# Attention scores laid out with keys on partitions, reduced over the keys by GpSimd

## The reference, cut to what matters

```python
def swa_sink_attention(q, k, v, sinks, rel_bias):
    # chunks of 64 queries; each reads its own and the previous chunk of 64 keys (a band of 128)
    logits = jnp.einsum('bnqkgd,bnskd->bnkgqs', q, kb).astype(jnp.float32)
    logits = logits * (1.0 / math.sqrt(HEAD_DIM)) + band_bias(rel_bias)[None, None]
    logits = jnp.where(valid[None, :, None, None, None, :], logits, NEG)
    sink = sinks.astype(jnp.float32).reshape(1, 1, N_KV_HEADS, GROUP, 1, 1)
    m = jnp.maximum(jnp.max(logits, axis=-1, keepdims=True), sink)
    p = jnp.exp(logits - m)
    denom = jnp.sum(p, axis=-1, keepdims=True) + jnp.exp(sink - m)
    p = (p / denom).astype(vb.dtype)
    o = jnp.einsum('bnkgqs,bnskd->bnqkgd', p, vb)
    return o.reshape(b_, s_, ATTN_WIDTH)
# afterwards: attn * silu(g_attn), next to conv * silu(g_conv), times w_out
```

## Time and profile before

| | |
|---|---|
| time, median of 3 runs | 1341.59 us (1341.4 to 1342.21) |
| the profiled execution | 1342.15 us, span 1340.4 us |
| PE busy | 1327.5 us, 99% of the span |
| DVE busy | 908.1 us, 68% |
| ACT busy | 543.5 us, 41% |
| POOL busy | 90.3 us, 7% |
| units of attention | 393 to 965 us of the span |

### The profile page before, as it was taken

One profiled execution on the slowest core, in us unless ns is written; L12 is line 12 of the kernel. 1 busy time (PEld: TensorE's weight loads), 2 busy tenths in 40 slices (PEclk: granted clock), 3 DMA queues, 4 the chain that ended last, 5 costly groups with the idle time before them and its releaser, 6 DMA issues.

```text
span 1340.4 us, 16528 instructions
## 1 busy us (share of the span) xinstructions
PE 1327.5 (99%) x6038; PEld 1099.2 (82%) x6038; DVE 908.1 (68%) x1132; ACT 543.5 (41%) x946; POOL 90.3 (7%) x151
## 2 busy tenths in 40 slices
PE   9999999999999999999999999999999999999997
PEld 8887888888888888888888888888888888888886
DVE  6899766323577449975589745997439896665376
ACT  7856532232233433434334333334323444321444
POOL 1222220000000000000000000000001121100001
PEclk9999999999999999999999999999999999999999
DMA  9779995988797998779987799787898978899768
GB/s 368 288 271 373 389 351 150 319 310 318 290 297 241 308 301 277 230 219 317 302 287 249 235 312 305 225 261 244 295 348 296 326 259 287 298 306 360 267 260 301
DMA packets 167888, 390.01 MB, mean 291 GB/s; under 512 B 77920, under 2 KB 90240, under 8 KB 146176
## 3 DMA queue, kind: packets, MB, share of 16 engines
q1 hardware_dynamic: 148272, 322.08, 71.7%
q0 software_dynamic: 18240, 62.92, 12.8%
q10 hardware_dynamic: 1296, 3.96, 0.8%
HBM read 294.18 MB, written 98.93 MB: 293 GB/s over the span
## 4 chain that ended last, share of the span: by engine, by line
PE 91%; DVE 6%; issue 2%; DMA 1%; ACT 0%; POOL 0%; POOLq 0%; DVEq 0%; ACTq 0%
PE banks L2009 86%; PE banks L2038 1%; PE banks L2050 1%; DVE x_main L1357 1%; DVE w_ring L1344 1%; DMA x_park<-e 1%; PE banks L1969 1%; PE banks L2059 1%; PE banks L2060 1%; DVE raw L1454 0%; PE banks L1994 0%; DVE raw L1442 0%; DVE e L1502 0%; DVE raw L1436 0%; DVE z L1466 0%
## 5 line engine op out<-in xcount | busy, mean ns | idle before, releaser
L2009 PE MATMUL banks<-x_main,w_ring 128*128 128x512 f32 x2352 | 551.0, 391 | 1.0 <-DVE e L1505 0.5
L2009 PEld LDWEIGHTS banks<-x_main,w_ring 128*128 128x128 f32 x2352 | 438.5, 188 | 91.9 <-issue 1.4
L970 ACT ACTIVATE w_ring<-raw 128x1024 fp32r<-128x1024 f32 x223 | 235.5, 1056 | 544.4 <-PE banks L2009 537.6
L1344 DVE TENSOR_TENSOR w_ring<-raw,w_ring 128x1024 fp32r<-128x1024 f32 x223 | 272.9, 1224 | 218.3 <-ACT w_ring L970 216.7
L2009 PE MATMUL banks<-x_far,w_ring 128*128 128x512 f32 x1680 | 393.4, 391 | 0.1
L2009 PEld LDWEIGHTS banks<-x_far,w_ring 128*128 128x128 f32 x1680 | 313.0, 188 | 64.7 <-DVE e L1502 0.5
L2009 PE MATMUL banks<-w_ring,x_main 128*128 128x512 f32 (+1 forms) x1020 | 230.9, 387 | 0.3 <-DVE e L1502 0.3
L2009 PEld LDWEIGHTS banks<-w_ring,x_main 128*128 128x128 f32 x1020 | 189.9, 188 | 39.6 <-DVE e L1502 0.7
L505 POOL DMA_DIRECT2D x_park<-x_main x104 | 56.1, 539 | 1006.0 <-DVE x_main L1357 1005.9
L1001 ACT ACTIVATE x_main<-z 128x512 fp32r<-128x512 f32 x104 | 64.9, 624 | 116.6 <-issue 81.5
L1357 DVE TENSOR_TENSOR x_main<-z,x_main 128x512 fp32r<-128x512 f32 x104 | 71.3, 687 | 37.7 <-ACT x_main L1001 37.5
(11 more groups left out here) (164 smaller groups left out, 845.3 us busy)
## 6 DMA issues: line engine op xcount, KB each, us to landing
x_far<-x_park SPq DMA_DIRECT2D x84, 1024.0 KB, 6.3
x_main<-x_park SPq DMA_DIRECT2D x84, 1024.0 KB, 6.1
raw<-in_w_blocks_dram SPq DMA_DIRECT2D x127, 512.0 KB, 5.4
x_park<-x_main POOLq DMA_DIRECT2D x104, 512.0 KB, 5.7
q_cur<-qkv_park SPq DMA_DIRECT2D x64, 128.0 KB, 4.9
z<-mix_park SPq DMA_DIRECT2D x16, 512.0 KB, 7.7
z<-in_x_dram SPq DMA_DIRECT2D x6, 1024.0 KB, 13.0
x_park<-e POOLq DMA_DIRECT2D x8, 512.0 KB, 6.4
```

What stands on the lines that cost most here:

```text
L970: act.activation(w_ring[:, n % NW, :, 0, :], raw[:, c, k:k + 2, :], ACT.Copy).then_inc(w_hi_ready, 1)
L1344: dve.tensor_tensor(w_ring[:, n % NW, :, 1, :], raw[:, c, k:k + 2, :], w_ring[:, n % NW, :, 0, :], ALU.subtract).then_inc(w_lo_ready, 1)
L2009: op = pe.matmul(bank, left, right, start=(first and i == 0), stop=(kt == HK - 1 and i == 2), skip_group_check=goes_on)
```

## The change

Scores are computed with the 128 keys on the partitions and 8 heads times 64 queries along the row (128x512), so the probabilities come out as the product with the values wants them, and the transposes on PE go. The maximum over the keys and the sum over the keys now run across partitions, by GpSimd's `partition_all_reduce`. The sink is a second block of 512 columns beside the scores. The output is not normalised through the probabilities: the gate is multiplied by the reciprocal of the sum, which DVE gets by transposing 32x32 blocks. The low part of the probabilities goes from DVE to POOL, ahead of the sum. The order by `o`: DVE scales at 1, POOL takes the maximum at 1, DVE shifts by it at 4, ACT takes the exponential at 5 and the high part at 6, POOL the low part and the sum at 5, DVE weights the gate at 11.

```diff
+        logits = [sb(f"logits{i}", [P, 2, N], Z + 4096 + 4096 * i) for i in range(KVH)]
+        probs = sb("probs", [P, 2, N], Z + 12288)
+        top = sb("top", [P, N], Z + 16384)
+        total = sb("total", [P, N], Z + 18432)
...
+            def key_max(u):
+                pool.wait_ge(logits_read, u + 1)
+                if u > 0:
+                    pool.wait_ge(shift_step, 2 * u)
+                pool.partition_all_reduce(top, logits[u % 2][:, 0, :], P, bass.bass_isa.ReduceOp.max).then_inc(max_ready, 1)
+
+            def split_p_lo(u):
+                pool.wait_ge(pt_hi_ready, u + 1)
+                pool.tensor_tensor(pt_lo[:, :], probs[:, 0, :], pt_hi[:, :], ALU.subtract).then_inc(pt_lo_ready, 1)
+
+            def key_sum(u):
+                pool.wait_ge(exp_done, u + 1)
+                if u > 0:
+                    pool.wait_ge(weight_step, 6 * u)
+                pool.partition_all_reduce(total, probs[:, 0, :], P, bass.bass_isa.ReduceOp.add).then_inc(key_sum_ready, 1)
...
+                act.wait_ge(shift_step, 2 * u + 2)
+                act.activation(probs[:, :, :], probs[:, :, :], ACT.Exp).then_inc(exp_done, 1)
...
+                act.activation(pt_hi[:, :], probs[:, 0, :], ACT.Copy).then_inc(pt_hi_ready, 1)
...
+            def scale_logits(u):
...
+                dve.scalar_tensor_tensor(out=logits[kv][rows, 0, :], in0=logit_ps[rows, :], scalar=SCALE,
+                                         in1=bias[rows, kv * PAIRS * 2:(kv + 1) * PAIRS * 2, :].rearrange("p h s -> p (h s)"),
                                          op0=ALU.mult, op1=ALU.add).then_inc(logits_read, 1)
...
+            def shift_logits(u):
...
+                dve.wait_ge(max_ready, u + 1)
+                dve.tensor_tensor(top, top, logits[kv][:, 1, :], ALU.max).then_inc(shift_step, 1)
...
+                dve.tensor_tensor(probs[:, :, :], logits[kv][:, :, :], top.unsqueeze(1).to_broadcast([P, 2, N]), ALU.subtract
+                                  ).then_inc(shift_step, 1)
+
+            def weight_gate(u):
+
+                dve.wait_ge(key_sum_ready, u + 1)
+                dve.tensor_tensor(total, total, probs[:, 1, :], ALU.add).then_inc(weight_step, 1)
+                dve.wait_ge(weight_step, 6 * u + 1)
+                dve.transpose(total_turned, total).then_inc(weight_step, 1)
+                dve.wait_ge(weight_step, 6 * u + 2)
+                dve.reciprocal(inv_turned, total_turned.rearrange("p (c t) -> p c t", t=32)[:, :, 0]).then_inc(weight_step, 1)
...
+                    dve.transpose(inv_row[rows, :].rearrange("p (j c t) -> p j c t", j=PAIRS, c=2),
+                                  mine.unsqueeze(3).to_broadcast([HEAD, PAIRS, 2, 32])).then_inc(weight_step, 1)
...
+                dve.tensor_tensor(g_cur[:, :, :], g_cur[:, :, :], inv_row.rearrange("p (j k) -> p j k", j=PAIRS), ALU.mult
+                                  ).then_inc(weight_step, 1)
...
-                for j in range(PAIRS):
-                    op = pe.matmul(logit_ps[:, j, :, :].rearrange("p c k -> p (c k)"),
...
+                pe.matmul(logit_ps, k_cur[:, 0, :], queries, start=True, stop=False)
+                pe.matmul(logit_ps, k_cur[:, 1, :], queries, start=False, stop=True).then_inc(qk_done, 1)
```

More of the change, by code:

```diff
@@ L922, in _ @@
                         store_park(PARK_AT[n, quarter])
+                    u, o = unit_at(n, quarter)
+                    if 0 <= u < UNITS:
+                        if o == 1:
+                            key_max(u)
+                        elif o == 5:
+                            split_p_lo(u)
+                            key_sum(u)
                 b, p, q = place(n + 2) if n + 2 < STEPS else (BLOCKS, 0, 0)
@@ L1554, in attention_setup @@
                 for kv in range(KVH):
-                    dve.memset(logits[kv][:, :, 0:CHUNK], -NEG).then_inc(edges_written, 1)
+                    dve.memset(logits[kv][0:CHUNK, 0, :], NEG).then_inc(edges_written, 1)
                 dve.wait_ge(rel_loaded, 48)
                 for kv in range(KVH):
[L1558 to L1561, removed]
+                    heads = slice(kv * PAIRS * 2, (kv + 1) * PAIRS * 2)
+                    dve.tensor_copy(logits[kv][:, 1, :].rearrange("p (h s) -> p h s", h=PAIRS * 2),
+                                    sink_row[:, heads].unsqueeze(2).to_broadcast([P, PAIRS * 2, CHUNK])
+                                    ).then_inc(edges_written, 1)
                 dve.memset(u_buf[:, :, 0:2], 0.0).then_inc(edges_written, 1)
-            def shift_logits(u):
+            def scale_logits(u):
                 kv = u % 2
@@ L1756, in _ @@
                         if o == 1:
+                            scale_logits(u)
+                        elif o == 3 and u % 2 == 0:
+                            turn_v_lo(u // 2)
+                        elif o == 4:
                             shift_logits(u)
[L1758 to L1761, removed]
-                                turn_v_lo(u // 2)
-                            turn_p_lo(u)
+                        elif o == 11:
+                            weight_gate(u)
                     if o == 3 and 0 < u <= UNITS:
                         gate_output(u - 1)
-                    late_w = CONV0 <= b < OUT0 and i in (0, 6) and unit_at(n, 2)[1] == 10 and unit_at(n, 2)[0] < UNITS
-                    if quarter == 2 and late_w:
-                        w_lo(n + 2)
                     if quarter == 1:
-                        if W_TABLED <= n + 2 < STEPS and not late_w:
+                        if W_TABLED <= n + 2 < STEPS:
                             w_lo(n + 2)
@@ L2081, in extras @@
                         queries_by_keys(u)
[L2082 to L2083 removed]
+                        if u % 2 == 0:
+                            turn_values(u // 2)
             pe.wait_ge(constants_made, 4)
```

140 lines of the change are left out of this document (58 added, 82 removed).

## The result

The changed kernel takes 1645.15 us (median of 4 runs, 1644.66 to 1646.73), against 1341.49 us for the kernel before on the same chip. The ratio is 1.2265, 95% interval 1.2244 to 1.2286: 304 us slower. The forecast was 1727 us, range 1560 to 1940.

The account below looks back on a forecast made before the run. PE bound the kernel at 17.87 us a unit; a POOL and DVE loop of 29.9 us would replace it, 12.0 us more, times 32 is 385 us, on 1342.15 us giving 1727 us, range 1560 to 1940.

Parts of the forecast that it names:

- The bound and the place: PE bounds the old kernel at 17.87 us a unit; only the units' stretch grows, 572 to about 950 us.
- the ring: In each unit POOL's maximum, low part and sum and DVE's gate and scale wait in a loop: 29.9 us.
- The reloads: POOL reloads its library ahead of the low part and the sum in every unit: 7.7 us each.
- The all-reduces: POOL's maximum and sum over the keys in each unit: 4.2 us each, between 1.2 and 8.4.
- The sum: Ring total per unit: POOL 25.0 us, DVE 4.2 us, four handovers 0.7 us, together 29.9 us.
- The chain beside the first reload: DVE and ACT work from POOL's maximum to its low part: 7.4 us, just hidden under the 7.7 us reload.
- DVE's work: DVE per unit loses 3.6 us and gains 5.4 us, going from 12.9 to 14.7 us.
- The port: Rival: reloads nearly free, POOL blocks DVE operations with two SBUF operands; 154 us more, 1496 us, chance 0.11.
- PE's gain: PE drops four transposes of the probabilities, 0.44 us a unit; 14.1 us in all, invisible behind the ring.
- The clock: Rival: PE's clock falls to 1.2 GHz in the waits, its unit takes 34.9 us; 1885 us, chance 0.04.
- the serial fold: Rival: POOL folds partitions one after another, 26.4 us an all-reduce, ring 74.3 us; 3150 us, chance 0.04.

Follow-up runs that it names:

- cutting the ring at the gate: Changed kernel with both reloads kept, DVE weighting the gate of unit u at o = 2 of unit u+1: 1534.45 us, ratio 1.1439.
- the 32 idle reloads: Kernel before plus idle POOL all-reduce, subtraction, all-reduce in every second unit, for which no compute engine waits: 1343.70 us, ratio 1.0013.
- the all-reduces that need none between them: Kernel before plus two idle POOL all-reduces in each unit, no reload between, no compute engine waiting: 1342.14 us, ratio 1.0003.
- the run without all-reduces: Changed kernel with the low part on DVE and both all-reduces replaced by POOL memsets of constants: 1344.58 us, ratio 1.0019.
- The run without reloads: Changed kernel with the low part made by DVE at o = 7, so no reload is left in the units: 1383.09 us, ratio 1.0307.
- the lean version: Changed kernel, low part on DVE, all-reduces kept, sink subtracted from bias once, ACT clipping the maximum, sum turned on 256 columns: 1356.38 us, ratio 1.0106.

## Why the prediction was right, step by step

**The bound and the place.** PE set the pace before, the units' stretch alone grew, and the time is that of a ring through POOL and DVE. Held: the new waits are those that the forecast named, and cutting the ring at the gate gave 111 us back.

**The reloads.** Taken as 7.7 us, between 0.18 and 13.0. Measured 8.4 us ahead of the sum and 7.4 us ahead of the low part, 8.3 us each where nothing waits. The gap of 0.18 us was indeed no switch. That 7.7 us came this near is luck: it is the time of a transfer of 512 KB, picked among three sizes, and no row shows such a transfer. The profile counts 167889 DMA packets with the 32 idle reloads and as many with the all-reduces that need none between them. The Trainium skill's figure of about 6 us for a freshly loaded kernel (GPSIMD Engine Reference, 2.1 Instruction dispatch) is short of these gaps by 1.4 to 2.4 us; its remark that no instruction in the profile shows it agrees with the rows: behind two records of under 0.1 us they say "issue".

**The all-reduces.** Taken as 4.2 us each, mis-sized: 2.7 us for the maximum and 3.25 us for the sum, 2.45 us less together. On its own, an all-reduce for a maximum takes 1.8 us (median). The other 0.9 us look like the port, in the ring this time: DVE's line 1367 had begun 0.18 us before the maximum of 723.63 us and ran to 724.67. The prediction also says that both ends of this term, 1.2 and 8.4 us, stay in the range; its own 1535 and 1996 us for them lie outside.

**The sum.** Turn by turn, from the groups: 2.7 + 7.4 + 1.5 + 8.4 + 3.25 = 23.2 us on POOL, forecast 25.0, and (308.6 - 171.2) / 31 = 4.4 us between sum and maximum (171.2 is the wait ahead of the first), forecast 4.9. That is 27.6 against 29.9 us. The 2.3 us, 32 times, are 74 of the 82 us by which the forecast was too high.

**The chain beside the first reload.** Forecast 7.4 us, to hide just under the reload. POOL's low part was released by "issue" 20 times and by ACT's `pt_hi` 12 times: on average they are as close as that. In the turn shown the chain was much shorter, 3.7 us (the maximum ended at 726.31 us, ACT's copy at 730.05), since DVE had done the work ahead of the shift during the maximum.

**DVE's work.** 14.7 us a unit, and 15.4 with the low part: the run without all-reduces has 15.4. The changed kernel itself has 502.22 / 32 = 15.7, so about 1 us a unit of it is waiting at the port.

**The port.** The mechanism is there, the price was wrong. 9.6 us a unit were put down as if an all-reduce held DVE from start to end. It does so only in its first part, and only what it meets: 17.6 - 15.4 = 2.2 us a unit. The Trainium skill's rule (SBUF — State Buffer, Who interferes with whom) has the second instruction block fully until the first ends; POOL's tensor-tensor operations agree, the all-reduce doesn't, since DVE was let go about 1.1 us before its end. As a rival it had 1496 us with free reloads, 154 us over the kernel before. The run without reloads took 1383 us, 41 us over: a rival right in kind, nearly four times too dear (of the 41 us, 38.5 go when the all-reduces do, their duration included).

**PE's gain.** Forecast 14.1 us and invisible. It is 18.6 us when nothing else is late: each unit lost 0.56 us rather than 0.44, so more went than the transposes' own time. The 72 matmuls of a unit's three steps took 10.93 + 5.49 = 16.42 us before and 16.34 here, and what stands between them 0.03 us less; why the 72 got faster isn't shown.

**The clock.** PE was granted 0.87 in the units' stretch, not 1.00. Its part stayed under the ring's, and from 715 to 760 us the chain of waits holds nothing of PE, so this decided nothing there; nor did the serial fold, which the 2.7 us rule out.

What isn't shown: what a reload does in its 8 us and why the gap ranges up to 11.3 us, and how much of the last 14 us of the lean version is blocking and how much DVE's own work in the stretches with the convolution.

## What to carry to other kernels

On GpSimd, ask of each pair of neighbouring instructions whether they live in the same library, and look in the built program for reloads: alternating cost 8 us a switch here, and it hurts where an engine waits for it. Then write down the ring: a helper engine whose input waits, in another engine's fixed order, for its own last output adds all its latencies to the pace, however idle it looks (POOL was busy for 20% of the span). And count the work that moves to the engine with the least slack: a gain of 14 to 19 us on PE was outweighed here by 2.5 us a unit on DVE and 2.2 us of waiting for the port.

## What the runs showed of the hardware that was not expected

- An all-reduce over 128 partitions of 512 float32 columns took 1.8 us for a maximum alone (on zeros, median) and 3.25 us for a sum.
- In the rows seen it excludes DVE's operations with two operands in SBUF only in its first part. At 725.66 us line 1647 multiplied two tiles of SBUF in its usual 0.42 us while an all-reduce (723.63 to 726.31 us) was still running (first row below). That end is firm: line 1604, which waited for it, started at 726.35 us.
- It works the other way too: an all-reduce that starts beside such an operation of DVE gets longer, 4.30 in place of 3.25 us for the sum and 2.68 in place of 1.8 us for the maximum.
- A DVE operation with one tile as input is held too: the first tap of the convolution takes 543 ns on average in the kernel before (second row) and 1068 ns in the one with the low part on DVE and the gate weighted late (third row), both in the units' stretch. Only some are held: of all 16 there the median is 544 ns and the longest 2464 ns.

```profile
725.66 0.42 DVE L1647 TENSOR_TENSOR o_mix<-o_mix,g_cur 128x256 f32<-128x256 f32 x1
```
```profile
L1633 DVE TENSOR_SCALAR y_buf<-u_buf,cols 128x512 f32<-128x512 f32 x14 | 7.0, 543 | 0.1
```
```profile
L1666 DVE TENSOR_SCALAR y_buf<-u_buf,cols 128x512 f32<-128x512 f32 x14 | 14.4, 1068 | 0.1
```
